# The first mixer of a two-part transformer: gelus moved into the projection, three program blocks made one, pooling sums on GpSimd

## The chip, the cores and the metric

The kernel runs on one core of one Trainium2 chip. The metric is the device time of one execution, in microseconds. The engines are TensorE (PE; its weight loads are shown as PEld), VectorE (DVE), ScalarE (ACT), GpSimd (POOL) and SyncE (SP), which here only issues DMAs.

## The reference

The program is a stack: two layers of a first model (modulated norm, a mixer, a "peer" feed-forward that picks experts), and one layer of a second model. Only the first layer's mixer is touched. Sequence length is 256 tokens, model width 1024, everything in float32. Cut to what matters here:

```python
def chunked_spatial_gating(u, v, w_s, b_s, g_v):
    vf = v.astype(jnp.float32)
    mu = jnp.mean(vf, axis=-1, keepdims=True)
    var = jnp.mean((vf - mu) ** 2, axis=-1, keepdims=True)
    vn = ((vf - mu) * lax.rsqrt(var + EPS) * g_v).astype(v.dtype)
    vn = vn.reshape(B, S // GM_CHUNK, GM_CHUNK, GM_GROUPS, GM_CH)
    w = jnp.where(causal[None], w_s, 0)
    sv = jnp.einsum('gts,bnsgc->bntgc', w, vn) + b_s.T[None, None, :, :, None]
    return u * sv.reshape(B, S, GM_WIDTH)

def multiscale_pool(p, w_pool, ls):
    ...
    for g, w in enumerate(POOL_WINDOWS):          # (2, 4, 8, 16)
        lag = cs_pad[:, POOL_MAXW - w:POOL_MAXW - w + S, sl]
        outs.append((cs[..., sl] - lag) / cnt - pf[..., sl])
    mixed = jnp.einsum('bsgc,gcd->bsgd', pooled, w_pool).reshape(B, S, POOL_WIDTH)
    return mixed * ls

# in first_block, layer 0:
mod = (c_act @ ada_w[l] + ada_b[l]).reshape(B, 6, D)[:, :, None, :]
sh1, sc1, g1, sh2, sc2, g2 = (mod[:, i] for i in range(6))
h = rmsnorm(x, norm_mix[l]) * (1 + sc1) + sh1
proj = h @ ev_w_in[e]
z = jax.nn.gelu(proj[..., :2 * GM_WIDTH], approximate=False)
ya = chunked_spatial_gating(z[..., :GM_WIDTH], z[..., GM_WIDTH:], ev_w_s[e], ev_b_s[e], ev_g_v[e])
yb = multiscale_pool(proj[..., 2 * GM_WIDTH:], ev_w_pool[e], ev_pool_scale[e])
y = jnp.concatenate([ya, yb], axis=-1) @ ev_w_out[e]
x = x + g1 * y
h = rmsnorm(x, norm_ffn[l]) * (1 + sc2) + sh2
x = x + g2 * peer(h, peer_w_q[l], peer_sub_keys[l], peer_u[l], peer_v[l])
```

The other layers compute the same as before, with the same instructions.

## The kernel before

Activations lie transposed, features on the 128 partitions and the 256 tokens along the free dimension, as 8 blocks of 128x256 (`x_T`). A big tensor `arena` holds what each stage needs. Weights are streamed in tiles of 128x1024 (512 KB) through a ring of four slots: SyncE issues the load of tile n+4 when TensorE has used tile n (`load_tile`, L249), ScalarE makes the rounded high part (`make_high`, L277), VectorE the remainder (`make_low`, L283), and TensorE multiplies with both parts. `linear` is this loop with hooks: `aside` is a generator of extra work for VectorE, one step a tile, `aside_act` the same for ScalarE, `issue` for DMAs that ScalarE issues, `behind` for loads that SyncE puts behind a given tile.

Every stage is an `nc.Block()`: one instruction stream for each engine. At its end all engines wait for each other, so a block lasts as long as its slowest engine, and nothing of the next block starts earlier. Inside a block the order on each engine is the order in which the code is written; semaphores (`wait_ge`, `then_inc`) order the engines among each other, and a `Chain` makes VectorE wait for its own instruction before.

The part of the program around the change is `even_mixer`, from 38 to 160 us:

1. `linear` over `ev_w_in`, 12 tiles. VectorE has one modulation block a tile as `aside` (a dot product of 1024 elements with the conditioning vector, L699, blocks 16 to 27). Their weights come in chunks of four blocks (2 MB each, L671): chunks 0 and 1 in the setup, chunks 2 and 3 issued behind tiles 5 and 7 of this linear.
2. A block with the gelus of u and v (L987, L988), the clearing of the gate table (8 MB of zeros written to DRAM by four DMAs, L745), the mean and variance by TensorE (L976, L981), a square root, the pooling windows (L1003 to L1014, nine instructions of adds and copies) and the mask on VectorE, a reciprocal (L1017) and the scaling of v (L1018). SyncE loads five small arrays, waits for all of them, and then issues chunks 4 and 5. Modulation blocks 28 and 29 stand first on VectorE.
3. A block (`token_major`) that turns the scaled v by eight transposes (L907), with modulation blocks 30 to 33 on VectorE.
4. A block with the spatial matmuls (L1031), the pooling matmuls (L1035), and their evictions into `cat` (L1044, L1047, L1054).
5. `linear` over `ev_w_out`, 8 tiles, with the sum of squares for the next norm and modulation blocks 34 to 39. After block 39 a bias add and a gain are computed (L684, L688).

The gate table is read and added to by the peer stage, which first needs it past 212 us. `keep_warm` issues matmuls of zeros.

## Time and profile before

| | us |
|---|---|
| runs | 2633.80, 2637.85, 2642.37 |
| median of the runs | 2637.85 |
| span of the profiled execution | 2641.4 |
| TensorE busy | 2431.8 (92%) |
| VectorE busy | 1854.0 (70%) |
| ScalarE busy | 1319.5 (50%) |
| GpSimd busy | 574.5 (22%) |

The profile gives the span, from the first to the last instruction, of one execution, and no total time of its own beside it; the slowest of the three runs is 0.97 us above that span. Times in rows are microseconds from the start of the span; the last of a row in brackets is how long the engine stood idle before it and whose event ended that. "PEq" as the releaser, with the line of a block, is the wait of all engines for each other at a block's end. A TensorE instruction in float32 on 128x256 shows as two records.

### The profile page before, as it was taken

What the parts mean: (1) busy time and instruction counts of PE and PEld (TensorE: products, weight loads), DVE (VectorE), ACT (ScalarE), POOL (GpSimd) and SP (SyncE); (2) the same over time, 40 slices, a digit from 0 to 9 for tenths busy, and PEclk for the clock granted to TensorE, in tenths of its full rate; (3) what the DMA queues carried; (4) which work ended last, traced back from release to release, by engine and by line L of the source; (5) the groups of instructions that cost most, each with busy time, mean ns of one, the idle gap of its engine ahead of it and who ended that gap; (6) DMA issues with size and microseconds to landing.
All of it is one profiled execution on the core that took longest, in us unless ns stands there. A gap on an engine that the chain in (4) does not pass through costs nothing. (4 is left out here: it accounts for less than half of the span.)

```text
span 2641.4 us, 44330 instructions
## 1 busy us (share of the span) xinstructions
PE 2431.8 (92%) x16488; PEld 2160.9 (82%) x16488; DVE 1854.0 (70%) x3808; ACT 1319.5 (50%) x2022; POOL 574.5 (22%) x392
## 2 busy tenths in 40 slices
...
GB/s 348 279 165 149 181 183 181 182 260 56 247 264 262 266 265 192 275 80 144 171 182 182 182 183 123 135 216 216 218 218 155 175 140 80 4 129 95 174 167 153
DMA packets 200513, 480.52 MB, mean 182 GB/s; under 512 B 54448, under 2 KB 87728, under 8 KB 199760
## 3 DMA queue, kind: packets, MB, share of 16 engines
...
## 5 line engine op out<-in xcount | busy, mean ns | idle before, releaser
L283 DVE TENSOR_TENSOR weight_low<-weight_raw,weight_high 128x1024 fp32r<-128x1024 f32 x732 | 893.6, 1223 | 375.2 <-ACT weight_high L277 365.1
L277 ACT ACTIVATE weight_high<-weight_raw 128x1024 fp32r<-128x1024 f32 x732 | 774.1, 1059 | 646.1 <-DMA weight_raw<-peer_v_dram 342.0
L387 PE MATMUL bank<-h_parts,weight_high 128*128 128x256 f32 x4608 | 842.7, 286 | 38.1 <-DVE h_parts L570 21.7
L387 PEld LDWEIGHTS bank<-h_parts,weight_high 128*128 128x128 f32 x4608 | 729.6, 195 | 40.3 <-issue 40.3
L387 PE MATMUL bank<-h_parts,weight_low 128*128 128x256 f32 x2304 | 657.8, 286 | 0.0
L1217 POOL DMA_INDIRECT gate_table<-pick_expo,pick_spot x256 | 475.3, 1857 | 594.4 <-DVE pick_expo L1319 379.9
L387 PEld LDWEIGHTS bank<-h_parts,weight_low 128*128 128x128 f32 x2304 | 448.6, 195 | 0.0
L394 PE MATMUL bank<-h_parts,weight_high 128*128 128x512 f32 x1120 | 400.5, 407 | 39.1 <-DVE weight_low L283 17.5
L1505 PE MATMUL bank<-weight_high,act_high 128*128 128x512 f32 x1024 | 316.0, 390 | 7.2 <-DVE act_low L1572 6.1
L1505 PE MATMUL bank<-weight_low,act_high 128*128 128x512 f32 x1024 | 315.3, 389 | 0.0
L1505 PE MATMUL bank<-weight_high,act_low 128*128 128x512 f32 x1024 | 315.2, 389 | 0.0
L396 PE MATMUL bank<-h_parts,weight_low 128*128 128x256 f32 x1120 | 297.5, 285 | 0.0
L394 PEld LDWEIGHTS bank<-h_parts,weight_high 128*128 128x128 f32 x1120 | 208.6, 193 | 91.7 <-issue 47.3
L1572 DVE TENSOR_TENSOR act_low<-arena,act_high 128x256 fp32r<-128x256 f32 x256 | 108.7, 425 | 213.1 <-ACT act_high L1539 213.0
L1505 PEld LDWEIGHTS bank<-weight_high,act_high 128*128 128x128 f32 x1024 | 191.9, 188 | 47.9 <-issue 8.4
L396 PEld LDWEIGHTS bank<-h_parts,weight_low 128*128 128x128 f32 x1120 | 217.0, 194 | 11.2
L1505 PEld LDWEIGHTS bank<-weight_low,act_high 128*128 128x128 f32 x1024 | 192.3, 188 | 40.0
L1505 PEld LDWEIGHTS bank<-weight_high,act_low 128*128 128x128 f32 x1024 | 192.3, 188 | 39.8
L1282 ACT ACTIVATE arena<-bank 128x256 f32<-128x256 f32 x256 | 97.9, 382 | 214.6 <-PE bank L387 214.1
L494 ACT ACTIVATE arena<-bank 128x256 f32<-128x256 f32 x140 | 53.2, 380 | 127.0 <-PE bank L394 126.3
L1539 ACT ACTIVATE act_high<-arena 128x256 fp32r<-128x256 f32 x256 | 102.2, 400 | 10.4 <-PEq L1368 9.6
L1661 POOL TENSOR_TENSOR arena<-arena,trig 128x512 f32<-128x512 f32 x4 | 5.4, 1380 | 467.6 <-POOLq L418 467.6
...
## 6 DMA issues: line engine op xcount, KB each, us to landing
weight_raw<-peer_u_dram SPq DMA_DIRECT2D x256, 512.0 KB
weight_raw<-peer_v_dram SPq DMA_DIRECT2D x256, 512.0 KB
...
gate_table<-kept ACTq DMA_DIRECT2D x8, 2048.0 KB, 17.4
...
kept<-gate_table SPq DMA_DIRECT2D x256, 64.0 KB, 3.4
...
```

The costliest lines, as they stand in the source:

```text
L277: self.nc.scalar.activation(self.high[:, slot, :], self.raw[:, slot, :], ACT.Identity) \
L283: eng.tensor_tensor(self.low[:, slot, :], self.raw[:, slot, :], self.high[:, slot, :].bitcast(F32), ALU.subtract) \
L387: mm = self.nc.tensor.matmul(out, w, x, start=(start and i == 0), stop=(stop and i == 2), skip_group_check=skip)
L394: wide = lambda: self.nc.tensor.matmul(bank[:], high, parts.rearrange("p s t -> p (s t)"), start=start, stop=stop, skip_group_check=True)
L396: narrow = lambda: self.nc.tensor.matmul(bank[:, 0:T], low, parts[:, 0, :], start=False, stop=False, skip_group_check=True)
L494: nc.scalar.activation(sums[:, n, :], self.bank[b][:, T:2 * T], ACT.Identity).then_inc(copied.sem, 1)
L1217: pool.indirect_dma_start(core.table[layer], bass.IndirectOffsetOnAxis(ap=b.spot[:, h, i:i + 1], axis=0), b.expo[:, 0, h, i:i + 1], None, ...
L1282: nc.scalar.activation(acts[:, n, :], core.bank[n % RING][:, 0:T], ACT.Gelu).then_inc(free.sem, 1)
L1505: mm = nc.tensor.matmul(out[2 * t + h][:], x[:, slot, of], w[:, slot, halves[h]], start=(first and n == 0), stop=(last and n == 2), skip_g ...
L1539: nc.scalar.activation(core.act_high[:, n % RING, :], acts[:, n, :], ACT.Identity).then_inc(rounded.sem, 1)
L1572: nc.vector.tensor_tensor(core.act_low[:, slot, :], acts[:, n, :], core.act_high[:, slot, :].bitcast(F32), ALU.subtract).then_inc(split.se ...
L1661: nc.gpsimd.tensor_tensor(dst[:, 2 * n:2 * n + 2, :], src[:, 2 * n:2 * n + 2, :], cosb, ALU.mult) \
```

## The change

In words:

- The first linear gets `gelus` as `aside_act`: eight gelus of 128x256, one a tile from tile 2 on, behind the copy and the high part of that tile. Each waits until VectorE has added that block. Chunk 3 is no longer loaded there.
- The three blocks behind it become one. GpSimd makes the pooling windows (two memsets, a copy and four adds). VectorE no longer copies windows, it multiplies by the counts straight from the two buffers (two instructions of 128x512). Square root and reciprocal become Ln and Exp with scale -0.5 on ScalarE. The first three weight tiles of `ev_w_out` are split into high and low parts in this block. Modulation blocks 28 and 29 stand behind the pooling work, 30 and 31 move on.
- SyncE loads the small arrays in two sets with no wait of its own, and issues chunks 3, 4 and 5 right behind.
- The second linear does not load the table for the root again (it was loaded in the block before), starts with the activations' parts at once, takes modulation blocks 30 and 31 before its tile loop (`early=2`) and one block behind each of its 8 tiles (32 to 39). ScalarE issues the clearing of the gate table there, 8 pieces of 1 MB, one a tile.
- The waits for the cleared table count the new number of DMAs. The second table is still cleared in four pieces.

The diff, cut to its core:

```diff
                     return
-                if squares is not None:
+                if squares is not None and not prepared:
                     self.prepare_root()
                 if halves is not None:
...
                 steps = iter(()) if aside is None else aside(dve)
+                for _ in range(early):
+                    next(steps, None)
                 for n in range(seg.count):
                     done = (n + 1) % groups == 0
...
+CLEARINGS = (8, 4)
+CLEARED = (16 * CLEARINGS[0], 16 * (CLEARINGS[0] + CLEARINGS[1]))
+
+
+def clearing(core, eng, layer):
+
+    parts = CLEARINGS[layer]
+    cleared, zeros = core.sig("table_cleared"), core.zeros.unsqueeze(1).to_broadcast([P, P * P // D // parts, D])
+    table = core.table[layer].rearrange("(p c n w) o -> c p n (w o)", p=P, c=parts, w=D)
     eng.wait_ge(core.sig("zeros_made").sem, layer + 1)
-    for c in range(CLEARINGS):
+    for c in range(parts):
         eng.dma_start(table[c], zeros).then_inc(cleared.sem, 16)
+        yield
 
 
...
+    def gelus(act):
+        yield
+        yield
+        for n in range(8):
+            act.wait_ge(free.sem, free.at(n + 1))
+            nc.scalar.activation(proj[:, n, :], proj[:, n, :], ACT.Gelu)
+            yield
+
     core.linear("scalar", None, sums=proj, aside=lambda dve: modulations(core, dve, range(16, 28)), norm=mixer_norm(core, 0),
-                behind={5: lambda sp: load_modulations(core, sp, 2), 7: lambda sp: load_modulations(core, sp, 3)})
+                behind={5: lambda sp: load_modulations(core, sp, 2)}, aside_act=gelus, prepare=False)
     u, v, p = proj[:, 0:4], proj[:, 4:8], proj[:, 8:12]
-    gelus = sig("gelus_ready")
...
+            for name, pairs in small_sets.items():
+                for dst, source in pairs:
+                    sp.dma_start(dst, core.dram[source]).then_inc(sig(name).sem, 16)
+            for q in range(3, 6):
                 load_modulations(core, sp, q)
 
         @block.tensor
         def _(pe):
...
                 mm = nc.tensor.matmul(var, core.c("ones"), squares[:, g, :], start=(g == 0), stop=(g == 3))
             mm.then_inc(vars_.sem, 1)
-            core.keep_warm(6)
+            core.keep_warm(3)
+            pe.wait_ge(normed.sem, normed.at(1))
+            for t in range(TT):
+                transposes(core, pe, [centred[:, g, t * P:(t + 1) * P] for g in range(4)], [core.bank[t]], turned)
+            core.keep_warm(1)
+            pe.wait_ge(masked.sem, masked.at(1))
+            for t in range(TT):
+                pe.wait_ge(kept.sem, kept.at(t + 1))
+                for g in range(4):
+                    mm = nc.tensor.matmul(core.bank[2 + t][:, g * P:(g + 1) * P], tokens[:, t, g * P:(g + 1) * P],
+                                          spatial[:, g, :], start=True, stop=True)
+                mm.then_inc(mixed.sem, 1)
+            pe.wait_ge(sig("pooling_loaded").sem, 48)
+            pe.wait_ge(pooling.sem, pooling.at(1))
+            for g in range(4):
+                mm = nc.tensor.matmul(core.bank[4 + g][:, 0:T], w_pool[:, g, :], pooled[:, g, :], start=True, stop=True)
+                mm.then_inc(pools.sem, 1)
...
-            nc.scalar.activation(v, v, ACT.Gelu).then_inc(gelus.sem, 1)
-            nc.scalar.activation(u, u, ACT.Gelu)
-            clear_table(core, act, 0)
+            core.prepare_root()
+            core.first_parts(act, "high")
...
-            nc.scalar.activation(root, var, ACT.Sqrt, bias=core.c("eps"), scale=1.0 / 512).then_inc(rooted.sem, 1)
+            nc.scalar.activation(root, var, ACT.Ln, bias=core.c("eps"), scale=1.0 / 512).then_inc(logged.sem, 1)
...
+        @block.gpsimd
+        def _(pool):
+            link = Chain(pool_step, pool)
+            nc.gpsimd.memset(ping[:, :, 0:16], 0.0)
+            nc.gpsimd.memset(pong[:, :, 0:16], 0.0)
+            link(nc.gpsimd.tensor_copy(ping[:, :, 16:], p))
+            src, dst = ping, pong
+            for g in range(4):
+                shift = 1 << g
+                i = nc.gpsimd.tensor_tensor(dst[:, g:4, 16:], src[:, g:4, 16:], src[:, g:4, 16 - shift:16 - shift + T], ALU.add)
+                if g < 3:
+                    link(i)
+                src, dst = dst, src
+            i.then_inc(windows.sem, 1)
...
+            core.first_parts(dve, "lows")
             dve.wait_ge(rooted.sem, rooted.at(1))
...
+            nc.vector.tensor_tensor(centred, centred, root.unsqueeze(1).to_broadcast(wide), ALU.mult).then_inc(normed.sem, 1)
+            dve.wait_ge(sig("spatial_loaded").sem, 32)
+            nc.vector.tensor_tensor(spatial, spatial, mask.unsqueeze(1).to_broadcast([P, 4, P]), ALU.mult).then_inc(masked.sem, 1)
+            dve.wait_ge(windows.sem, windows.at(1))
+            dve.wait_ge(sig("pooling_loaded").sem, 48)
+            counts = inv_count.rearrange("p (g t) -> p g t", g=4)
+            for first, sums in ((0, pong), (1, ping)):
+                i = nc.vector.tensor_tensor(pooled[:, first:4:2, :], sums[:, first:4:2, 16:], counts[:, first:4:2, :], ALU.mult)
+            link(i)
+            nc.vector.tensor_tensor(pooled, pooled, p, ALU.subtract).then_inc(pooling.sem, 1)
+            for _ in modulations(core, dve, range(28, 30)):
+                pass
...
-                aside=lambda dve: modulations(core, dve, range(34, 40)), squares=core.x, root=core.work[:, 0:T])
+                aside=lambda dve: modulations(core, dve, range(30, 40)), squares=core.x, root=core.work[:, 0:T], prepared=True, early=2,
+                issue=lambda act: clearing(core, act, 0))
```

What stands in the order of instructions. First VectorE between the counts of the pooling and the block that evicts the spatial products, before (L1013 and L1014 are pooling, L1015 the mask, L1017 the reciprocal, L1018 the scaling of v, L699 modulation blocks, the branches with a barrier the ends of blocks):

```order
L1013 TENSOR_TENSOR arena<-arena 128x1024 [waits small_loaded,dve_step]
L1014 TENSOR_TENSOR arena<-arena 128x1024 [waits dve_step]
L1015 TENSOR_TENSOR arena<-arena 128x512 [waits dve_step]
L1017 RECIPROCAL work<-work 128x256 [waits rooted,dve_step]
L1018 TENSOR_TENSOR arena<-arena,work 128x1024 [waits dve_step]
L964 UNCONDITIONAL_BRANCH [waits dve_step]
L937 UNCONDITIONAL_BRANCH [waits barrier_Pool_Activation_PE_DVE_SP_release]
L699 SCALAR_TENSOR_TENSOR arena,mod<-arena,kept 128x1024 [waits mod_chunk3_loaded] x2
L699 SCALAR_TENSOR_TENSOR arena,mod<-arena,kept 128x1024 [waits mod_chunk4_loaded] x2
L922 UNCONDITIONAL_BRANCH
L1038 UNCONDITIONAL_BRANCH [waits barrier_Pool_Activation_PE_DVE_SP_release]
```

and VectorE of the changed kernel from the centring of v on (L1059; L1061 squares, L283 the low parts of `ev_w_out`, L1064 the scaling of v, L1066 the mask, L1071 and L1073 pooling, L706 modulation blocks 28 and 29, L1079 the eviction of the spatial products):

```order
L1059 SCALAR_TENSOR_TENSOR arena<-bank,arena 128x1024 [waits mean_ready]
L1061 TENSOR_TENSOR arena<-arena 128x1024 [waits dve_step]
L283 TENSOR_TENSOR weight_low<-weight_raw,weight_high 128x1024 [waits high_ready] x3
L1064 TENSOR_TENSOR arena<-arena,work 128x1024 [waits rooted]
L1066 TENSOR_TENSOR arena<-arena 128x512 [waits spatial_loaded]
L1071 TENSOR_TENSOR arena<-arena 128x2x256 [waits pooling_loaded,windows_summed]
L1071 TENSOR_TENSOR arena<-arena 128x2x256
L1073 TENSOR_TENSOR arena<-arena 128x1024 [waits dve_step]
L706 SCALAR_TENSOR_TENSOR arena,mod<-arena,kept 128x1024 [waits mod_chunk3_loaded] x2
L1079 SCALAR_TENSOR_TENSOR arena<-bank,cols,arena 128x128 [waits spatial_mixed]
L1079 SCALAR_TENSOR_TENSOR arena<-bank,cols,arena 128x128 x3
L1079 SCALAR_TENSOR_TENSOR arena<-bank,cols,arena 128x128 [waits spatial_mixed]
```

The low parts have moved ahead of the scaling, pooling and two modulation blocks stand between the scaling and the eviction, and there is no barrier between them.

Next ScalarE from the last eviction of the mixer into the second linear, before:

```order
L1054 ACTIVATE arena<-bank,cols 128x256 [waits pool_mixed] x4
L1026 UNCONDITIONAL_BRANCH
L512 UNCONDITIONAL_BRANCH [waits barrier_Pool_Activation_PE_DVE_SP_release]
L348 ACT_TABLE_LOAD
L277 ACTIVATE weight_high<-weight_raw 128x1024 [waits slot0_loaded]
L525 ACTIVATE h_parts<-arena 128x2x256 x4
L277 ACTIVATE weight_high<-weight_raw 128x1024 [waits slot1_loaded]
L277 ACTIVATE weight_high<-weight_raw 128x1024 [waits slot2_loaded]
L277 ACTIVATE weight_high<-weight_raw 128x1024 [waits slot3_loaded]
L326 ACTIVATE squares<-x_T 128x256 [waits bank_free]
L277 ACTIVATE weight_high<-weight_raw 128x1024 [waits slot0_loaded]
L326 ACTIVATE squares<-x_T 128x256 [waits bank_free]
```

and in the changed kernel:

```order
L1037 ACTIVATE arena<-bank,cols 128x256 [waits pool_mixed] x4
L987 UNCONDITIONAL_BRANCH
L513 UNCONDITIONAL_BRANCH [waits barrier_Pool_Activation_PE_DVE_SP_release]
L527 ACTIVATE h_parts<-arena 128x2x256 x4
L277 ACTIVATE weight_high<-weight_raw 128x1024 [waits slot3_loaded]
L326 ACTIVATE squares<-x_T 128x256 [waits bank_free]
L754 DMA gate_table<-kept 128x2x1024 [waits zeros_made]
L277 ACTIVATE weight_high<-weight_raw 128x1024 [waits slot0_loaded]
L326 ACTIVATE squares<-x_T 128x256 [waits bank_free]
L754 DMA gate_table<-kept 128x2x1024
L277 ACTIVATE weight_high<-weight_raw 128x1024 [waits slot1_loaded]
L326 ACTIVATE squares<-x_T 128x256 [waits squares_added,bank_free]
```

The table load and the first high parts are gone from the start, and a DMA that clears a piece of the table stands behind each tile's squares.

Last VectorE at the end of the second linear, before (L335 adds squares, L635 updates x, L283 is a low part of the next linear's weights):

```order
L699 SCALAR_TENSOR_TENSOR arena,mod<-arena,kept 128x1024 [waits mod_chunk5_loaded]
L684 TENSOR_TENSOR mod<-mod,cols 128x16 [waits mod_step]
L688 SCALAR_TENSOR_TENSOR gain<-mod,cols 128x8 [waits mod_step]
L335 TENSOR_TENSOR work<-work,squares 128x256 [waits squares_added,squared,mod_step]
L635 SCALAR_TENSOR_TENSOR x_T<-bank,mod,x_T 128x256 [waits tiles_used]
L283 TENSOR_TENSOR weight_low<-weight_raw,weight_high 128x1024 [waits high_ready]
L335 TENSOR_TENSOR work<-work,squares 128x256 [waits squares_added,squared]
L635 SCALAR_TENSOR_TENSOR x_T<-bank,mod,x_T 128x256 [waits tiles_used]
L283 TENSOR_TENSOR weight_low<-weight_raw,weight_high 128x1024 [waits high_ready]
L418 UNCONDITIONAL_BRANCH
```

and in the changed kernel (the same are L335, L642 and L283):

```order
L706 SCALAR_TENSOR_TENSOR arena,mod<-arena,kept 128x1024 [waits mod_chunk5_loaded]
L335 TENSOR_TENSOR work<-work,squares 128x256 [waits squares_added,squared]
L642 SCALAR_TENSOR_TENSOR x_T<-bank,mod,x_T 128x256 [waits tiles_used]
L283 TENSOR_TENSOR weight_low<-weight_raw,weight_high 128x1024 [waits high_ready]
L706 SCALAR_TENSOR_TENSOR arena,mod<-arena,kept 128x1024 [waits mod_chunk5_loaded]
L335 TENSOR_TENSOR work<-work,squares 128x256 [waits squares_added,squared]
L642 SCALAR_TENSOR_TENSOR x_T<-bank,mod,x_T 128x256 [waits tiles_used]
L283 TENSOR_TENSOR weight_low<-weight_raw,weight_high 128x1024 [waits high_ready]
L706 SCALAR_TENSOR_TENSOR arena,mod<-arena,kept 128x1024 [waits mod_chunk5_loaded]
L691 TENSOR_TENSOR mod<-mod,cols 128x16 [waits mod_step]
L695 SCALAR_TENSOR_TENSOR gain<-mod,cols 128x8 [waits mod_step]
L419 UNCONDITIONAL_BRANCH [waits mod_step]
```

A modulation block now follows each of the last two tiles, and the bias add and the gain (L691, L695) are the last instructions of the block.

## Rows read from the trace of the kernel before

**Rows 1.** Windows view: length, busy PE, PEld, DVE, ACT, POOL; granted clock, DMA share, GB/s.

```profile
86.40:108.00 21.60, 12.77 (x32) 7.30 (x32) 16.82 (x22) 5.04 (x5) 0.00 (x0) 0.82 0.99 384
...
129.40:159.50 30.10, 28.24 (x198) 26.06 (x198) 25.80 (x41) 14.26 (x21) 0.00 (x0) 0.90 0.45 140
```

**Rows 2.** Timeline of TensorE, 86 to 129.5 us: start, length, instruction, idle before.

```profile
88.83 3.78 PE L976 MATMUL bank<-arena,const 128*128 128x256 f32 x8 [5.13 <-ACT arena L987]
...
95.18 1.99 PE L981 MATMUL bank<-arena,const 128*128 128x256 f32 x8 [0.73 <-DVE arena L1001]
...
117.75 3.75 PE L1031 MATMUL bank<-arena 128*128 128x128 f32 x16 [7.58 <-PEq L922]
...
129.38 0.55 PE L387 MATMUL bank<-h_parts,weight_high 128*128 128x256 f32 x1 [5.12 <-DVE h_parts L570]
```

**Rows 3.** Timeline of VectorE, 70 to 125 us.

```profile
70.87 1.23 DVE L283 TENSOR_TENSOR weight_low<-weight_raw,weight_high 128x1024 fp32r<-128x1024 f32 x1 [2.35 <-ACT weight_high L277]
...
92.65 1.22 DVE L999 SCALAR_TENSOR_TENSOR arena<-bank,arena 128x1024 f32<-128x1024 f32 x1 [3.81 <-PE bank L976]
...
106.46 1.22 DVE L1018 TENSOR_TENSOR arena<-arena,work 128x1024 f32<-128x1024 f32 x1
...
115.07 1.22 DVE L699 SCALAR_TENSOR_TENSOR arena<-arena,kept 128x1024 f32<-128x1024 f32 x1 [4.46 <-DMA arena<-ada_first_dram]
...
122.71 1.23 DVE L1047 TENSOR_TENSOR arena<-arena 128x1024 f32<-128x1024 f32 x1
```

**Rows 4.** Windows view in stretches of 2 us: the granted clock.

```profile
84.00:86.00 2.00, 0.00 (x0) 0.00 (x0) 2.00 (x4) 0.11 (x1) 0.00 (x0) 0.98 0.37 119
86.00:88.00 2.00, 0.00 (x0) 0.00 (x0) 1.70 (x5) 1.57 (x2) 0.00 (x0) 0.50 0.77 185
...
92.00:94.00 2.00, 2.00 (x6) 1.03 (x4) 1.32 (x2) 0.78 (x1) 0.00 (x0) 0.82 1.02 353
```

**Rows 5.** Groups of instructions on GpSimd, kept apart by shape.

```profile
L1798 POOL TENSOR_TENSOR arena<-arena,trig 128x512 f32<-128x512 f32 x8 | 12.6, 1605 | 0.0
...
L1661 POOL TENSOR_TENSOR arena<-arena,trig 128x512 f32<-128x512 f32 x4 | 5.4, 1380 | 467.6 <-POOLq L418 467.6
...
L2405 POOL COPY arena<-const 128x64 f32<-128x64 f32 x16 | 3.8, 235 | 67.2 <-ACTq L2379 67.2
...
L840 POOL MEMSET kept<- 128x1024 f32 x1 | 1.0, 951 | 0.3 <-POOLq L2906 0.3
```

**Rows 6.** Groups on VectorE, 1090 to 1110 us, beside L1798 on GpSimd.

```profile
L1825 DVE TENSOR_TENSOR arena<-arena,scratch 128x512 f32<-128x512 f32 x8 | 8.6, 1076 | 0.7 <-POOL arena L1798 0.4
L1820 DVE TENSOR_TENSOR scratch<-bank,trig 128x512 f32<-128x512 f32 x8 | 5.4, 679 | 0.0
```

**Rows 7.** One line, L1364, from 600 to 612 us: durations min/median/max, first start.

```profile
L1364 POOL TENSOR_SCALAR scratch<-const,by_pick x4: 835/855/974, 604.1 to 606.8; 128x128 f32<-128x128 f32 x4
L1364 POOLq MODIFY_POOL_CONFIG  x2: 11/12/12, 604.0 to 604.0; - x2
```

**Rows 8.** Timeline of ScalarE, 124 to 140 us.

```profile
125.02 1.28 ACT L348 ACT_TABLE_LOAD   x1 [0.26 <-PEq L1026]
...
137.97 1.06 ACT L277 ACTIVATE weight_high<-weight_raw 128x1024 fp32r<-128x1024 f32 x1 [2.61 <-DMA weight_raw<-ev_w_out_dram]
```

**Rows 9.** DMA issues, 84 to 130 us: size each, median us to landing.

```profile
gate_table<-kept ACTq DMA_DIRECT2D x4, 2048.0 KB, 19.6
arena<-ada_first_dram SPq DMA_DIRECT2D x2, 2048.0 KB, 18.3
...
arena<-ev_w_pool_dram SPq DMA_DIRECT2D x1, 256.0 KB, 11.0
```

**Rows 10.** Timeline of VectorE, 151 to 160 us.

```profile
153.71 0.17 DVE L688 SCALAR_TENSOR_TENSOR gain<-mod,cols 128x8 f32<-128x8 f32 x1
...
156.12 0.48 DVE L635 SCALAR_TENSOR_TENSOR x_T<-bank,mod,x_T 128x256 f32<-128x256 f32 x1
158.02 1.23 DVE L283 TENSOR_TENSOR weight_low<-weight_raw,weight_high 128x1024 fp32r<-128x1024 f32 x1 [1.43 <-ACT weight_high L277]
```

112 lines of the change are left out of this document (43 added, 69 removed).

## The prediction

> **What bounds the kernel now.** I read the windows view by stage first, then TensorE's, VectorE's and ScalarE's timelines of the stretch, then the DMA issues; the chain of waits of the page holds only the last instruction and is of no use. Over the whole span TensorE is the bound, but not here: from 86.4 to 108.0 us it is busy 12.77 of 21.60 us, much of it with matmuls of zeros [rows 1]. The reader is to see three waits in TensorE's timeline: 5.13 us for the gelus, 7.58 us in front of the spatial matmuls, 5.12 us before the second linear starts [rows 2]. What ends them is a serial chain through blocks that end with a wait of all engines. In the first block VectorE is the chain from 92.65 (centring) to 107.7 (end of the scaling of v), without a gap [rows 3]. In the second, TensorE's transposes are long done, but VectorE waits 4.46 us for chunk 4 of the modulation weights, until 115.07 [rows 3]: chunks 4 and 5 took 18.3 us to land, since they were issued behind small loads that SyncE waited for, and beside the 8 MB of zeros, which took 19.6 us a piece [rows 9]. The third block is evictions and one multiply that ends at 123.9 [rows 3]. The second linear then loads a table and makes high and low parts before TensorE starts at 129.38 [rows 2, 8]. So every microsecond off this chain is a microsecond off the program: nothing runs beside it that could be late, since all later stages start behind it, and the weights of the next tiles lie in their slots.
>
> **The change part by part.** All times are from the barrier B that opens the mixer's block (86.4 before).
>
> (a) The first linear. Chunk 3, 2 MB, no longer stands in SyncE's queue ahead of tile 8. VectorE waited 2.35 us for that tile's high part at 70.87 [rows 3]; from there on it has about 2.9 us of work a tile and regains the time only until TensorE's own pace binds, which it does on the last tiles. I take 0.6 us, bounds 0 and 1. The eight gelus (about 0.4 us each, the size of a 128x256 activation) and one table load of 1.28 us [rows 8] stand on ScalarE, which in this stretch waits for DMAs and for TensorE each tile; their own wait, for a block added two tiles ago, is met. Nothing queued behind them (a copy and a high part) is needed for some microseconds. Cost 0; if that cover were gone it would be the 1.28 us.
>
> (b) The mixer, B to the next barrier, 38.6 us before (86.4 to 125.0 [rows 8]). The chain now: TensorE starts 0.3 behind B instead of behind table load and gelu. Eight records of 128x256 take 1.99 us at the high clock and 3.78 at the low one [rows 2]. The granted clock was 0.98 until 86 us and 0.50 right after, with TensorE idle since before 84, and on its way back only in the stretch from 92, at 0.82 [rows 4]; the new block opens just there, so I take the low level (1.2 GHz): mean at 4.1. Centring 1.22 [rows 3], 5.4. Then five instructions with two operands in SBUF: squares 1.22, three low parts 1.2 each, scaling 1.22, mask 0.69, with gaps 6.7 us. GpSimd works beside them. Its adds of 128x512 took 1.38 to 1.61 us [rows 5]; the four adds are 4, 3, 2 and 1 times 256 columns, five such halves, 6.9 to 8.0 us. The copy of 1024 columns is not in the trace: below lies the memset of that size, 0.95 us, above 16 times the copy of 64 columns, 3.8 us [rows 5]; I take 2.0, nearer the memset, since a copy of 64 columns is mostly fixed cost. With memsets and waits the windows are ready at about 11.2, bounds 8.5 and 13.5. While GpSimd adds, VectorE's adds with two operands in SBUF took 1.08 us instead of 0.69, and those with one in PSUM stayed at 0.68 [rows 6]. I take a half more for the time of overlap, 5.4 to 11.2, which costs 1.9 us (0 to 3.5): mask ends at 14.0. The root is no part of it: variance and Ln and Exp are ready some 2 us before the low parts end. GpSimd's windows, at 11.2, are awaited at 14.0 and hidden; past that point they are late one for one. Counts twice 0.69 and subtraction 1.22: 16.7. Modulation blocks 28 and 29, 2.6 us: 19.3; before, they stood in TensorE's wait for the gelus, now on the chain. Their chunk and the small arrays ahead of it are 3.4 MB; at the 384 GB/s of that stretch [rows 1], with 2 us of latency, they are there at about 11. TensorE's transposes, ScalarE's two copies and the spatial matmuls (3.75 us at the low clock [rows 2]) are done at about 17 and fit beside it. Evictions 2.3, memset and multiply 1.35: 22.9; barrier about 0.3: 23.2. Gain 15.4 us. Bounds: high clock, no contention and a short copy 19.3, gain 19.3; windows at 17 and low clock 26, gain 12.
>
> (c) Start of the second linear, 125.02 to 129.38, 4.36 us. Table load 1.28, high part 1.06 and low part 1.22 are out of the chain; barrier, one pair of high and one of low parts of the activations stay, 1.6 us. Gain 2.8 (2.3 to 3.0).
>
> (d) End of the second linear. A modulation block (1.22 and its accumulator read, 1.3 us) now follows tile 6 too, and the bias and gain (0.17 each, 0.45 with their waits [rows 10]) leave the place before it: x of tile 7, at 156.12, comes 0.85 later. Behind the low part at 158.02 [rows 10] come one more block and the bias and gain, 1.8 us, in which only the barrier waits. Loss 2.7 (1.9 to 3.2).
>
> (e) The table's 8 MB of zeros are written beside this linear, 1 MB a tile, with 0.5 MB of weights a tile. A tile takes TensorE about 3 us (198 records in 28.24 us, 24 a tile, the first at the low clock [rows 1]); 1.5 MB in 3 us is 0.5 MB a microsecond, where queues that were never empty moved 0.38 [rows 1]. So weights land later: the high part of tile 4 waited 2.61 us for its DMA at 137.97 as it was [rows 8]. With half the bandwidth a tile lands 1 to 1.5 us later. TensorE has tiles in hand and does not stop, but VectorE's low parts shift, and with them the last update. Loss 0.8; below 0, above 5: a load of 256 KB beside the zeros took 11.0 us [rows 9], and eight weight tiles late like that would stop TensorE about twice.
>
> (f) The wait for the cleared table comes past 212 us, long after the last piece, issued before 160 and 20 us at most in landing [rows 9]: 0. The rest of the program is unchanged.
>
> Before GpSimd's first add the changed program has an instruction that configures GpSimd, as the kernel before has in front of L1364. There it took 12 ns, and the first instruction behind it started 0.1 us later [rows 7]. The Trainium skill, page "GPSIMD Engine Reference", section "Instruction dispatch", states that the first call into a freshly loaded kernel pays about 6 us with nothing in the profile. By that rule the windows would be ready at 17 instead of 11, 3 us after VectorE asks; by the row nothing is lost. The row decides, and the rule is a rival below.
>
> The sum: -0.6 - 15.4 - 2.8 + 2.7 + 0.8 = -15.3 us. Against the profiled execution: span 2641.4 becomes 2626.1. Against the median of the runs, 2637.85, which lies 4.5 below the slowest of them, the one nearest to the profile's span: 2622.5.
>
> **The rivals.**
> 1. GpSimd becomes the bound of the block: windows not at 11 but at 17, if VectorE slows the adds as they slow it: 8.0 us times 1.08 over 0.69 is 12.5, and the copy at its upper bound 3.8, with 0.5 for the rest [rows 5, 6]. For it: adds of one size took between 1.38 and 1.61 [rows 5]. Against: three microseconds of margin. Price 3 us beyond 14.0, time 2625.5; with windows at 20, 2628.5. The rule quoted above would give this case.
> 2. The zeros starve the weights. For it: 11.0 us for 256 KB [rows 9]. Against: that load stood behind 1.3 MB of others and beside pieces of 2 MB issued all at once, not one a tile. Price 5 us more than taken, and 2 more at the start of the next linear: 2629.5.
> 3. The block is better than I sum it: the high clock at its start, 1.8, and no contention, 1.9: 2618.8.
> 4. Slower than before: GpSimd's four adds, each waiting for the last, take so long that windows come later than B + 29.5. The place is VectorE's wait before the counts; it decides from 14.0 and eats the whole gain at 29.5. It would need adds at over three times the 1.61 us a half. Only a slow strided or offset operand would do that: the offset of 1 to 8 columns is in no row. Windows at 35 give 2643.5.
>
> **How the numbers follow.** Forecast 0.63, rival 1 0.12, rival 2 0.12, rival 3 0.10, rival 4 0.03. The bounds of the terms sum to -23 at best (1, 19.3, 3.0, less 1.9 and less 0, is 21.4, with a wobble of the median) and to -6 at worst (12 and 2.3, less 3.2 and 5); the runs themselves differ by 8.6 us, and a median of a few by perhaps 3. Range 2614 to 2632. What a measurement of this kernel can tell from no change is 0.3%, 7.9 us, so faster means below 2629.9: the forecast, rival 3, rival 1 but for its tail, and half of rival 2 lie there: 0.86. Same 0.11, slower 0.03.
>
> **What would show it.** In the changed profile: the mixer's block takes 23 us and has one barrier; TensorE's first mean matmul starts 0.3 us behind it at a granted clock of 0.5; the low parts in that block take 1.5 to 1.8 us each while GpSimd adds and 1.2 after; VectorE does not wait before the counts; the second linear's first matmul comes 1.6 us behind its barrier; its last instruction on VectorE is the gain. The forecast is wrong if GpSimd's last add ends over 14 us behind B, if TensorE waits for a low part in the second linear, or if the stretches behind 160 us have changed by more than 2 us in sum.

## The result and the profile after

The changed kernel took 2624.85 us (median of 7 runs, 2614.69 to 2629.70), the kernel before 2639.64 us beside it (7 runs, 2632.20 to 2645.57). The ratio is 0.9939 with a 95% interval of 0.9922 to 0.9957: 16 us or 0.6% faster (the medians differ by 14.8 us). The forecast was 2622.5 us. Timed again on another chip the ratio was 0.9942 (0.9922 to 0.9962). Ratios compare fast runs alone: one of the eight runs of e1_clear_later below took 3075.94 us at a granted clock of 0.74 and does not count in its ratio.

First the windows view of the changed kernel, for the mixer's block and for the second linear up to VectorE's first instruction of the next one; the columns are those of [rows 1].

```profile
84.60:105.30 20.70, 15.19 (x60) 10.46 (x60) 18.28 (x24) 7.98 (x13) 8.05 (x7) 0.89 0.97 366
106.80:143.70 36.90, 29.34 (x198) 26.60 (x198) 28.32 (x47) 12.71 (x20) 0.00 (x0) 0.90 0.86 338
```

The block takes 20.7 us where three blocks took 38.6. The second linear takes 37.0 us, against 30.5 from its first matmul at 129.38 [rows 2] to the next linear, and moves 338 GB/s where it moved 140 [rows 1]. The gain and the price stand in these two rows. VectorE's first instruction of the next linear, before and changed, gives the end of both:

```profile
159.88 0.88 DVE L588 SCALAR_TENSOR_TENSOR arena<-x_T,gain,work 128x256 f32<-128x256 f32 x2 [0.63 <-PEq L418]
```

```profile
143.77 0.88 DVE L593 SCALAR_TENSOR_TENSOR arena<-x_T,gain,work 128x256 f32<-128x256 f32 x2 [0.97 <-PEq L419]
```

TensorE's timeline of the changed kernel:

```profile
84.62 1.97 PE L999 MATMUL bank<-arena,const 128*128 128x256 f32 x8 [2.32 <-PEq L419]
...
90.45 3.64 PE L1004 MATMUL bank<-arena,const 128*128 128x256 f32 x8 [2.14 <-DVE arena L1061]
...
106.79 0.77 PE L387 MATMUL bank<-h_parts,weight_high 128*128 128x256 f32 x2 [4.83 <-DVE h_parts L574]
...
127.39 0.48 PE L387 MATMUL bank<-h_parts,weight_high 128*128 128x256 f32 x2 [1.20 <-DVE weight_low L283]
```

The waits of 5.13 and 7.58 us [rows 2] are gone. The mean took 1.97 us, at the high level of the clock (2.4 GHz; granted 1.00 from 84 to 90 us), the variance 3.64 at the low one (1.2 GHz; granted 0.50 from 92 to 94 us). At 127.39 TensorE stands still for a low part, which the prediction had excluded.

VectorE's timeline of the block (L1059 centres v, L1061 squares it):

```profile
86.63 1.22 DVE L1059 SCALAR_TENSOR_TENSOR arena<-bank,arena 128x1024 f32<-128x1024 f32 x1 [2.31 <-PE bank L999]
87.89 2.51 DVE L1061 TENSOR_TENSOR arena<-arena 128x1024 f32<-128x1024 f32 x1
90.32 4.86 DVE L283 TENSOR_TENSOR weight_low<-weight_raw,weight_high 128x1024 fp32r<-128x1024 f32 x3
95.10 1.21 DVE L1064 TENSOR_TENSOR arena<-arena,work 128x1024 f32<-128x1024 f32 x1
96.24 0.68 DVE L1066 TENSOR_TENSOR arena<-arena 128x512 f32<-128x512 f32 x1
96.84 1.28 DVE L1071 TENSOR_TENSOR arena<-arena 128x512 f32<-128x512 f32 x2
...
103.78 1.23 DVE L1082 TENSOR_TENSOR arena<-arena 128x1024 f32<-128x1024 f32 x1
```

It never waits after the mean. The squares take 2.51 us instead of 1.22 and the three low parts 4.86 instead of 3.5. GpSimd's part, first its timeline, then three views of the line of the adds (durations in ns: least, median, most, then the first and last start):

```profile
84.76 1.04 POOL L1044 COPY arena<-arena 128x1024 f32<-128x1024 f32 x1
85.87 7.09 POOL L1048 TENSOR_TENSOR arena<-arena 128x1024 f32<-128x1024 f32 x4
```

```profile
L1048 POOLq MODIFY_POOL_CONFIG  x2: 12/12/12, 85.7 to 85.8; - x2
L1048 POOL TENSOR_TENSOR arena<-arena x1: 1897/1897/1897, 85.9 to 85.9; 128x1024 f32<-128x1024 f32 x1
L1048 POOL TENSOR_TENSOR arena<-arena x2: 1466/1682/1897, 85.9 to 87.8; 128x1024 f32<-128x1024 f32 x1, 128x768 f32<-128x768 f32 x1
L1048 POOL TENSOR_TENSOR arena<-arena x2: 1588/1746/1905, 89.4 to 91.4; 128x512 f32<-128x512 f32 x1, 128x256 f32<-128x256 f32 x1
```

The windows are ready at 92.96, 8.4 us behind the barrier; VectorE takes them at 96.84. The adds of 1024 and 768 columns last 1.90 and 1.47 us, those of 512 and 256 last 1.91 and 1.59: the smaller ones are waiting for something. Read beside VectorE's rows it is turn-taking. The squares come at 87.89, the add of 768 columns has begun at 87.83 and ends at 89.3, and the squares end 1.1 us behind that. The add of 512 comes at 89.4, and ends 0.9 us behind the squares' end at 90.4; the first low part comes at 90.32 and ends at 92.38, 1.1 us behind the add. The pattern goes on to the last add.

The second linear on VectorE, its waits and one whole tile (132.10 to 134.77):

```profile
117.12 1.23 DVE L283 TENSOR_TENSOR weight_low<-weight_raw,weight_high 128x1024 fp32r<-128x1024 f32 x1 [1.93 <-ACT weight_high L277]
...
120.83 1.23 DVE L283 TENSOR_TENSOR weight_low<-weight_raw,weight_high 128x1024 fp32r<-128x1024 f32 x1 [0.61 <-ACT weight_high L277]
...
126.02 1.22 DVE L283 TENSOR_TENSOR weight_low<-weight_raw,weight_high 128x1024 fp32r<-128x1024 f32 x1 [2.08 <-ACT weight_high L277]
...
129.47 1.23 DVE L283 TENSOR_TENSOR weight_low<-weight_raw,weight_high 128x1024 fp32r<-128x1024 f32 x1 [0.36 <-ACT weight_high L277]
...
132.10 0.48 DVE L642 SCALAR_TENSOR_TENSOR x_T<-bank,mod,x_T 128x256 f32<-128x256 f32 x1
132.49 1.21 DVE L283 TENSOR_TENSOR weight_low<-weight_raw,weight_high 128x1024 fp32r<-128x1024 f32 x1
133.62 1.22 DVE L706 SCALAR_TENSOR_TENSOR arena<-arena,kept 128x1024 f32<-128x1024 f32 x1
134.77 0.08 DVE L706 DVE_READ_ACCUMULATOR arena<-arena,kept 128x1 f32 x1
134.77 0.42 DVE L335 TENSOR_TENSOR work<-work,squares 128x256 f32<-128x256 f32 x1
135.10 0.48 DVE L642 SCALAR_TENSOR_TENSOR x_T<-bank,mod,x_T 128x256 f32<-128x256 f32 x1
...
138.11 0.48 DVE L642 SCALAR_TENSOR_TENSOR x_T<-bank,mod,x_T 128x256 f32<-128x256 f32 x1
140.02 1.23 DVE L283 TENSOR_TENSOR weight_low<-weight_raw,weight_high 128x1024 fp32r<-128x1024 f32 x1 [1.43 <-ACT weight_high L277]
```

From 132.10 to 135.10 and on to 138.11, a tile takes VectorE 3.0 us without a gap; three matmuls of TensorE take 0.36 us here, 24 of them 2.9. VectorE has no slack left to make up a wait. The kernel before has the same 3.0 us in each tile with a modulation block, between two low parts of its second linear:

```profile
142.08 1.22 DVE L283 TENSOR_TENSOR weight_low<-weight_raw,weight_high 128x1024 fp32r<-128x1024 f32 x1
...
145.09 1.21 DVE L283 TENSOR_TENSOR weight_low<-weight_raw,weight_high 128x1024 fp32r<-128x1024 f32 x1
```

In the changed kernel the high parts wait for weights, on ScalarE, 11.5 us in four times:

```profile
ACT weight_high L277 <- DMA weight_raw<-ev_w_out_dram: 11.5, 4, 3.8
```

and the windows view shows the load on the DMA engines (share 1.02, 418 GB/s), and an idle stretch ahead of it:

```profile
106.00:108.00 2.00, 1.21 (x6) 1.24 (x7) 2.00 (x4) 2.00 (x4) 0.00 (x0) 0.50 0.17 70
108.00:110.00 2.00, 2.00 (x11) 2.00 (x11) 2.00 (x4) 0.43 (x1) 0.00 (x0) 0.50 0.00 0
...
116.00:118.00 2.00, 2.00 (x19) 2.00 (x19) 0.88 (x1) 1.37 (x2) 0.00 (x0) 1.00 1.02 418
```

The DMA view, for three single microseconds (114 to 115, 116 to 117, 118 to 119), tells the two queues apart; q1 carries the weights, q10 the zeros (packets, MB, share of the 16 DMA engines):

```profile
q1 hardware_dynamic: 75, 0.31, 90.3%
...
q10 hardware_dynamic: 101, 0.41, 100.4%
...
q1 hardware_dynamic: 102, 0.40, 97.6%
```

Here the two do not share the bandwidth evenly, they take turns: the weights of tile 5, issued at 114.70, move hardly anything before the piece of zeros issued at 112.36 is through.

### The profile page after: what moved, and what is told of

Read it like the earlier page. It is cut to its first block and busy times, and to the rows that moved or that the text cites. A ratio compares the mean times of both kernels' runs of the same rounds, so it can differ in the third digit from the quotient of the medians.

```text
span 2622.7 us, 44309 instructions
## 1 busy us (share of the span) xinstructions
PE 2425.7 (92%) x16484; PEld 2155.7 (82%) x16484; DVE 1850.0 (71%) x3797; ACT 1319.6 (50%) x2028; POOL 580.2 (22%) x399
## 5 line engine op out<-in xcount | busy, mean ns | idle before, releaser
L283 DVE TENSOR_TENSOR weight_low<-weight_raw,weight_high 128x1024 fp32r<-128x1024 f32 x732 | 894.8, 1225 | 367.8 <-ACT weight_high L277 363.4
```

Source lines behind the costliest of these rows:

```text
L283: eng.tensor_tensor(self.low[:, slot, :], self.raw[:, slot, :], self.high[:, slot, :].bitcast(F32), ALU.subtract) \
```

## The experiments

Three lengths serve below, all from the profiled executions: the block (barrier to the second linear's start), the second linear (first matmul to VectorE's first instruction of the next linear), and the next linear from there to the first scores. Behind the scores nothing differs but the run: an unchanged stretch behind the first layer's table, from GpSimd's L1364 to its memset past 1066 us (lines of the kernel before), varied between 481 and 489 us, so effects of 1 to 3 us are read from stages.

| kernel | block | second linear | next linear | all, to the scores |
|---|---|---|---|---|
| before | 40.86 | 30.50 | 52.88 | 126.34 |
| changed | 20.70 | 36.98 | 52.91 | 112.09 |
| changed, again | 20.97 | 36.55 | 53.25 | 112.27 |
| e1_clear_later | 20.97 | 33.06 | 58.18 | 113.71 |
| e2_no_adds | 19.53 | 37.02 | 53.65 | 111.70 |
| e3_early4 | 20.87 | 35.04 | 54.25 | 111.66 |
| e4_mods_first | 19.94 | 36.35 | 52.92 | 110.71 |
| e6_front_loaded | 20.97 | 36.31 | 53.63 | 112.41 |
| e7_front_early4 | 20.71 | 34.43 | 53.10 | 109.74 |
| e8_vector_windows | 23.44 | 35.42 | 53.59 | 113.95 |
| e9_zeros_323 | 20.97 | 35.19 | 54.04 | 111.70 |
| e10_zeros_early4 | 20.97 | 33.84 | 53.17 | 109.48 |
| e11_before_late | 35.41 | 33.69 | 51.92 | 123.11 |
| e12_zeros_in_block | 30.39 | 35.96 | 52.82 | 120.67 |

The last column also holds the start of the second linear (1.5 us; 2.1 where it loads a table). For before and e11 the block ends with the first high part, so that the table load of 1.28 us and 1 us of weight part are in it; counted to the barrier it was 38.6.

**The zeros one linear later (e1_clear_later).**

```
-                aside=..., prepared=True, early=2, issue=lambda act: clearing(core, act, 0))
+                aside=..., prepared=True, early=2)
...
 (peer-query linear)
-                    aside=lambda dve: angles(...), per_tile=3, norm=ffn_norm(core, layer))
+                    aside=lambda dve: angles(...), per_tile=3, norm=ffn_norm(core, layer),
+                    issue=lambda act: clearing(core, act, 0))
```

> The changed kernel, with the clearing of the first gate table moved from the second linear to the peer-query linear behind it (8 pieces of 1 MB, one behind each of its first 8 of 16 tiles). In the changed kernel the second linear takes 37.0 us from its first matmul (106.8) to the next linear's first instruction on VectorE (143.8), 30.5 before. Theory A, the zeros hold up the weights: the high parts' waits for DMA in that linear go back to about 1 to 2.6 us, TensorE does not stop in it, and it takes 33.0 to 33.5 us; the peer-query linear has more slack and loses at most 1 us; in all 3 us faster than the changed kernel. Theory B, VectorE bounds it, with a modulation block behind every tile: it stays at 36 to 37 us. Theory C, the zeros cost the same wherever weights stream: 3.7 us back there, 3 to 4 lost in the next linear, total within 1 us of the changed kernel.

Timed 2632.80 us against 2641.66 before, ratio 0.9960 (0.9946 to 0.9973). The second linear fell to 33.06 us: the zeros cost 3.9 us there (3.5 against the second profile of the changed kernel). VectorE waits for one high part behind the start, where the changed kernel has four such waits:

```profile
117.35 1.23 DVE L283 TENSOR_TENSOR weight_low<-weight_raw,weight_high 128x1024 fp32r<-128x1024 f32 x1 [1.20 <-ACT weight_high L277]
```

But the next linear rose by 4.9 to 5.3 us. The waits view of ScalarE in that linear, first of this kernel, then of the changed one (us, times, longest):

```profile
ACT weight_high L277 <- DMA weight_raw<-peer_w_q_dram: 22.3, 12, 3.4
```

```profile
ACT weight_high L277 <- DMA weight_raw<-peer_w_q_dram: 6.4, 11, 2.0
```

So the zeros are no cheaper there: theory A held for the second linear, theory C for the sum.

**Without GpSimd's adds (e2_no_adds).** The four adds are left out, and with them the pooling's window sums; a copy of one column takes their place.

```
-            for g in range(4): ... nc.gpsimd.tensor_tensor(dst..., src..., src shifted, ALU.add)
+            i = nc.gpsimd.tensor_copy(pong[:, :, 16:17], p[:, :, 0:1])
```

> The changed kernel with GpSimd's four window adds left out (a copy of one column a group stands in for them, so the pooling half of the mixer is not computed). Theory A, GpSimd and VectorE hold each other up when both read two operands from SBUF: VectorE's squares fall from 2.51 to 1.22 us, the three low parts from 4.86 to 3.5 us, and the scaling of v starts 2 to 2.6 us earlier, then bounded by the low parts or by the root. Theory B, the squares are slow for another reason (high parts on ScalarE, DMA traffic): 2.51 stays. In all, the mixer's block falls from 20.7 to about 18.3 us by A.

VectorE's timeline, and TensorE's:

```profile
90.02 1.23 DVE L1056 TENSOR_TENSOR arena<-arena 128x1024 f32<-128x1024 f32 x1
91.17 3.49 DVE L283 TENSOR_TENSOR weight_low<-weight_raw,weight_high 128x1024 fp32r<-128x1024 f32 x3
```

```profile
85.27 3.45 PE L999 MATMUL bank<-arena,const 128*128 128x256 f32 x8 [2.32 <-PEq L419]
```

Squares 1.23 and low parts 3.49: what VectorE loses in the block is GpSimd's doing, 2.65 us in the first profile. In the second profile it is 1.3 us, and e2 is to be compared with that one: in both the mean fell into the low clock. There the block shrank from 20.97 to 19.53 us, 1.4, and not to the 18.3 expected.

**Four modulation blocks ahead (e3_early4).** `early=2` becomes `early=4`.

> The changed kernel with four modulation blocks ahead of the second linear's tile loop instead of two; so none stands behind its last two tiles, as before the change. Theory A, the tail is what the last block, the bias add and the gain cost: from the last update of x to the next linear's first instruction on VectorE 5.66 us falls to 3.8, and the last update itself moves by at most 0.9 us, since late weights set its time; first matmul to next linear 37.0 to 35. Theory B, the two blocks only move: VectorE, 2.6 us later at tile 0, hands low part 3 on late and TensorE stops; 37.0 stays within 0.5.

The stage fell by 1.5 to 1.9 us, to the 35.0 expected, and the next linear gave back 1.0 to 1.3, where VectorE waited longer for high parts (7.6 us against 6.2 and 6.6). Median not timed; the profiled run was 2622.94.

**Modulation blocks 28 and 29 first (e4_mods_first).** They go back in front of the centring, their chunk back into the first linear.

```
-                behind={5: lambda sp: load_modulations(core, sp, 2)}, ...
+                behind={5: ..., 7: lambda sp: load_modulations(core, sp, 3)}, ...
 (VectorE, ahead of the wait for the mean)
+            for _ in modulations(core, dve, range(28, 30)): pass
```

> The changed kernel with chunk 3 loaded behind tile 7 of the first linear again and modulation blocks 28 and 29 first in the mixer's block, as before the change. Theory A: the two blocks, 2.6 us, fill VectorE's wait of 2.31 us for the mean and leave the chain: the mixer's block falls from 20.7 to about 18.5 us; the first linear ends 0.8 us later relative to its first tile. Theory B, with them VectorE's squares come under GpSimd's adds for longer, or the mean is late anyway, and less than 1 us is won; and the chunk costs the first linear 2 us or more.

GpSimd's and VectorE's timelines:

```profile
85.85 1.99 POOL L1044 COPY arena<-arena 128x1024 f32<-128x1024 f32 x1
87.92 8.80 POOL L1048 TENSOR_TENSOR arena<-arena 128x1024 f32<-128x1024 f32 x4
```

```profile
85.72 1.23 DVE L706 SCALAR_TENSOR_TENSOR arena<-arena,kept 128x1024 f32<-128x1024 f32 x1 [0.30 <-PEq L419]
86.87 2.05 DVE L706 SCALAR_TENSOR_TENSOR arena<-arena,kept 128x1024 f32<-128x1024 f32 x1
...
91.67 6.13 DVE L283 TENSOR_TENSOR weight_low<-weight_raw,weight_high 128x1024 fp32r<-128x1024 f32 x3
```

The block wins 0.8 to 1.0 us, not 2.2: the blocks fill the wait, but they take turns with GpSimd too. The copy comes at 85.85, behind a modulation block that runs to 86.9, and ends 1.04 us behind it at 87.84; the second modulation block ends 1.1 us behind that. Up to the block 0.9 us is lost in the first linear, where the chunk stands in the queue again, so nothing is won up to the block's end. Up to the scores the single profile is 0.5 us ahead with that loss counted in, too little to tell.

**Zeros into the idle stretch (e6_front_loaded), and with four blocks ahead (e7_front_early4).** Both timed with the changed kernel (e5_after_again) on one chip.

```
+            for _ in range(4): next(pieces)       # ScalarE, behind the copies of the tokens
...
-                issue=lambda act: clearing(core, act, 0))
+                issue=spread)                     # one piece at tiles 1, 3, 5, 7
```

> The changed kernel itself once more, timed on the same chip as the three kernels beside it. Expected: 2625 us, 14 to 18 us below the kernel before; the second linear 37 us from its first matmul to VectorE's first instruction of the next linear, that linear 53 us to the scores. It is the yardstick for what is won or lost below, and it shows by how much an unchanged stage differs from run to run.

> All 8 MB of zeros stay between the mixer's block and the end of the second linear, but four of the eight pieces are issued by ScalarE inside the mixer's block, behind its two copies of the tokens, so that they fall into the stretch of 106 to 114 us in which the DMA engines stood idle; the other four follow at every second tile. Theory A (the loss of the second linear is a queue of 1 MB of zeros a tile beside 0.5 MB of weights, and not the zeros as such): with half as many a tile the bandwidth suffices, ScalarE's waits for weights shrink from 13.2 us to under 5, and the second linear falls from 37.0 to 33.5 to 34.5 us, the next linear stays at 53: 2.5 to 3.5 us below the changed kernel timed beside it. Theory B (the rival: any zeros in front of the weights delay them, here those of the first tiles, which VectorE needs for its low parts at once): the waits only move to the first tiles, the stage stays at 36.5 to 37.5 and the time within 1 us. Theory C: the four early pieces delay chunks 4 and 5 of the modulation weights, and the block becomes longer than 21.5 us.

> The zeros as in the run before this one, and four modulation blocks instead of two ahead of the second linear's tile loop. With only the latter, the stage lost 1.9 us and the next linear gave 1.3 back, since the DMA queues bounded both. Theory A (the low parts of the next linear were late only since the zeros had pushed the weights back): with the queue relieved both add up: second linear 32 to 33 us, next one 53, 4 to 5 us below the changed kernel. Theory B (the next linear is bound by its own weights whatever is in front): again 1 to 1.5 us given back there, and a total within 1 us of the run before.

The changed kernel again 2625.92 us (8 runs), e6 2628.16 (9 runs, ratio to before 0.9952, 0.9936 to 0.9968), e7 2623.15 (6 runs, 0.9942, 0.9919 to 0.9965): these medians don't tell the three apart. In the stages e6 won nothing. ScalarE's and VectorE's timelines of e6:

```profile
119.85 1.06 ACT L277 ACTIVATE weight_high<-weight_raw 128x1024 fp32r<-128x1024 f32 x1 [5.65 <-DMA weight_raw<-ev_w_out_dram]
```

```profile
120.94 1.23 DVE L283 TENSOR_TENSOR weight_low<-weight_raw,weight_high 128x1024 fp32r<-128x1024 f32 x1 [4.32 <-ACT weight_high L277]
```

The other tiles waited for nothing (but for the last low part, 1.43 us in every kernel). One wait of 4.3 us in place of four with 5.0 in sum, and the stage was as long: rival theory B holds. The wait is for the weights of tile 4, issued at 113.25; from 113 to 117 us the queue of the zeros took 97% of the DMA engines and that of the weights 5%. With two more modulation blocks ahead of the tile loop (e7) the stage fell to 34.4 and the next linear gave nothing back: x of the last tile came only 0.4 us earlier, since the wait was still 3.84 us, and the tail behind it was 1.4 shorter. That is 2.4 to 2.5 us below the changed kernel, half of the 4 to 5 expected.

**Windows on VectorE (e8_vector_windows).** The copy and the four adds, with the same operands, stand on VectorE behind the mask.

> The one block stays, but the copy and the four adds of the pooling windows stand on VectorE again, behind the mask; GpSimd does its two memsets alone. It prices GpSimd's part. Theory A (GpSimd saves VectorE 4.1 us of windows and costs it 2.6 in slower squares and low parts, of which the wait for the root would keep 1.2): squares at 1.2 us, three low parts at 3.5, the block 23.4 us if the mean is taken at the high clock and 24 at the low one, against 20.7. Theory B (the slowing costs as much as the windows save): 20.7 or less. Stages behind it unchanged, 37.0 and 53.

The block took 23.44 us, near theory A, which had 24 for the mean at the low clock, as it was here. The second linear took 35.4, 1.1 to 1.6 less, so that GpSimd's part is worth 2.5 to 2.7 us in the block and 1.7 to 1.9 up to the scores.

**Zeros placed by what waits (e9_zeros_323), and with four blocks ahead (e10_zeros_early4).** As e6 and e7, with three pieces early, one at each of the tiles 1, 3, 5 and two behind the last.

> The eight pieces of zeros are placed by what VectorE waits for: three in the mixer's block, behind the two copies of the tokens (3 MB for the idle stretch of the DMA engines before the weights of tile 3 are issued), one behind each of the tiles 1, 3 and 5, two behind the last tile, where the next linear's weights are in their slots. Theory A (VectorE has 3.0 us of work a tile here, as TensorE has, so that each of its waits adds to the stage one for one, and the run with four early pieces only gathered the waits of four tiles into one of 4.3 us at tile 3, since 2 MB of zeros were still ahead of its weights at 113): now tile 3 waits 1.2 to 2 us and the others not at all, the second linear takes 33.2 to 34 us instead of 36.5 to 37, the next one 53: 2.5 to 3.3 us below the changed kernel (2625.9 on the last chip). Theory B (total bytes decide, wherever the pieces stand): the stage stays at 36 to 37. Theory C: the two last pieces delay the peer keys and the next linear's weights, and it gives back 1 us or more there.

> The same placing of the zeros, and four modulation blocks ahead of the tile loop, two of them in the time in which VectorE waits for tile 3. Theory A: both add, the second linear 31.5 to 32.5 us, the next one 53 to 53.5, 4.5 to 5 us below the changed kernel: about 2621. Theory B (the next linear's low parts, bound by their weights, take the gain back): as the run beside it, within 1 us.

e9 took 2627.59 us (5 runs, ratio 0.9961, 0.9947 to 0.9975), e10 2624.50 (6 runs, 0.9938, 0.9922 to 0.9954). The low part of tile 4 (the expectations count it as tile 3) still waited 2.74 us in e9 and that of tile 6 0.40; the stage fell by 1.4 to 1.8, half of what was expected, and the next linear gave back 0.8 to 1.1. In e10 the sum to the scores is 109.48, 2.6 to 2.8 us below the changed kernel where 4.5 to 5 were expected, the best of the stages measured; the medians can't show so little.

**The kernel before with only the zeros moved (e11_before_late).**

```
 (mixer's first block)
-            clear_table(core, act, 0)
 (second linear)
+                issue=lambda act: clearing(core, act, 0))
```

> The kernel before, with one thing alone of the change: the first table's clearing stands no longer in the mixer's first block, but in the second linear, eight pieces of 1 MB, one a tile. It tells what the zeros' place is worth by itself. Theory A: VectorE's wait of 4.46 us for chunk 4 of the modulation weights goes and the stretch from the mixer's block to the second linear's start falls from 38.6 to 34.2 us; in the second linear the zeros make VectorE wait for high parts 3.8 us in sum, of which one idle tile of VectorE (it has 6 modulation blocks for 8 tiles) takes up 1.2 to 2.5: the stage rises from 30.5 to 32 or 33; net 2 to 3 us won. Theory B (VectorE's slack takes up all): 30.5, net 4.4 won. Theory C (the zeros cost as much there as in the block): net 0.

The wait of 4.46 us for chunk 4 went; the block fell by 5.45 us, the second linear rose by 3.19, with VectorE waits for high parts of 1.74, 0.62 and 2.06. Net 3.2 up to the scores, a little more than theory A's 2 to 3. Its single run lasted 2648.70 us, longer than before's median of 2639.18; at the scores it was 3.0 us ahead of the profile of before, at the end 5.5 behind, and the stages between have the same instructions.

**The changed kernel with the zeros in the block (e12_zeros_in_block).**

```
 (mixer's block, ScalarE)
             core.first_parts(act, "high")
+            for _ in clearing(core, act, 0): pass
```

> The changed kernel with its eight pieces of zeros issued all at once near the start of the mixer's block, where the kernel before had them. It tells what the later place is worth inside the change. Until the block's end at B + 21 the DMA engines then have 16 MB in their queues, 38 us at 420 GB/s, beside 3.4 MB of small arrays and chunk 3. Theory A (the two queues share evenly, as in the kernel before): the small arrays and chunk 3 land at 16 to 19 us behind the barrier instead of 8 to 11, VectorE waits 1 to 4 us in the block for the counts or chunk 3, and chunks 4 and 5 and the weights of tile 3 come late in the second linear: block 22 to 25 us against 20.7 to 21.0, second linear 36 to 39 against 36.6 to 37.0, from block to scores 1 to 6 us longer than the changed kernel's 112.1 to 112.3. Theory B (what the zeros cost later they cost no more here, since the linear is relieved of them): block to scores within 1 us of 112.2. Theory C (as C, with the block covered by its own chain): shorter than the changed kernel by 1 to 3 us.

All three theories set it too low: 8.4 to 8.6 us more up to the scores, and the block is 9.4 to 9.7 us longer. ScalarE's and VectorE's timelines:

```profile
90.18 8.24 ACTq L754 DMA_DIRECT2D gate_table<-kept  x4
98.46 0.47 ACT L1031 ACTIVATE work<-bank,const 128x256 f32<-128x256 f32 x1 [8.00 <-issue]
```

```profile
99.42 1.23 DVE L1066 TENSOR_TENSOR arena<-arena,work 128x1024 f32<-128x1024 f32 x1 [2.61 <-ACT work L1033]
...
110.62 1.22 DVE L706 SCALAR_TENSOR_TENSOR arena<-arena,kept 128x1024 f32<-128x1024 f32 x1 [6.91 <-DMA arena<-ada_first_dram]
```

VectorE waits 6.91 us for chunk 3, and 2.61 for a root that ScalarE could have begun at 94.1: it was still issuing zeros, four pieces in 8.24 us. The second linear, free of new zeros, is hardly shorter (35.96): VectorE waits 4.86 us in it for the high part of tile 4.

## Why the prediction was right, step by step

The direction, the size and the place were right: 15.3 us forecast, 16.1 gone at the start of the next linear (159.88 to 143.77), of which 1.0 was there ahead of all edits. But that the size fits so well is luck: the block won 2.5 us more than forecast, the zeros cost 3.1 more, and the two cancelled. Two of the three signs that the prediction named for being wrong came: TensorE waited for low parts in the second linear (1.20 and 0.35 us), and the stretches behind 160 us changed by 2.6 us. The first belongs to (e), the second to (f). The third did not: the last add ends 8.4 us behind B, the barrier that opens the mixer's block.

(a) First linear: 0.6 forecast. The 2.35 us wait is gone and VectorE ends 1.84 us earlier, of which 1.0 is there already at ScalarE's first copy (49.56 against 48.54), ahead of all edits: 0.8. VectorE's work in a tile there is 2.6 us (its low parts in a row start 2.61 apart), not the 2.9 that the prediction took; TensorE's pace of 2.8 is what binds.

(b) The mixer's block: 15.4 forecast, 17.9 measured (17.6 in the second profile). Mean and clock: the forecast had the mean ready at B + 4.1 at the low clock; the first profile had it at 2.0. That was luck of the run: in ten other runs the mean took 3.16 to 3.65 us, and then the variance 1.99. TensorE pays for the low clock once, at one place or the other. The block hardly feels it (20.70 against 20.97): what the earlier mean won in the first profile, 1.6 us, VectorE lost again for the most part to GpSimd's adds, of which more were then still to come. Contention: 1.9 forecast, 2.65 measured in the first profile, 1.3 in the second (squares 2.00, low parts 4.01). Windows: ready at B + 8.4 against 11.2, since the copy took 1.04 us against 2.0, nearer still to the memset [rows 5], and the add of 128x512 took 1.04 in the second profile, where it began 0.1 us ahead of the squares and they waited for it, against 1.38 to 1.61 [rows 5]. Being hidden, this brought nothing. The mask ended at B + 12.3 (12.6 in the second profile) against 14.0. The rest of the difference is that I added durations: 1.22 us instructions of VectorE that do not depend on each other start 1.14 apart, as the three low parts in 3.49 us show, and I put gaps of 0.04 beside them. Of the 2.5 us by which the block beat the forecast (23.2 less 20.7) the mean is 2.1, contention takes back 0.8, and this leaves about 1.2 us for the overlap of some twenty instructions.

(c) Start of the second linear: 2.8 forecast, 2.86 measured (4.36 to 1.50).

(d) End of the second linear: loss 2.7 forecast. The zeros out of the way (e1), x of tile 7 comes 27.39 us behind the first matmul against 26.74, 0.65 (0.85 forecast), and the tail from there on 5.67 against 3.76, 1.9 (1.8 forecast).

(e) The zeros: loss 0.8 forecast, 3.9 measured by e1 (3.5 by the second profile). This is the mis-sized term, and it was wrong twice. First the weights: "with half the bandwidth a tile lands 1 to 1.5 us later". From SyncE's issue to the high part the tiles 4 to 7 took 3.5 us each before and in e1; in the changed kernel they took 4.2, 5.0, 7.3 and 7.9. They stand behind whole pieces of zeros, and the lateness grows from tile to tile. Then the price: the step saw that the low parts shift, but counted this once. VectorE's waits for high parts add up to 5.0 us, 3.8 more than the 1.20 of e1, and each stays, because with a modulation block behind every tile VectorE works 3.0 us a tile against TensorE's 2.9. The slack could have been worked out: low part, modulation block, update of x and sum of squares take 3.0 us in the tiles of before. e6 is the test: a single wait of 4.32 us, 3.1 more than e1's, and a stage 3.25 us longer. In all nine profiles with two blocks ahead of the tile loop x of the last tile comes 25.0 to 25.2 us behind the first matmul, plus VectorE's waits for high parts and for TensorE. In the kernel before, with two tiles free of a modulation block, the zeros still cost 3.2 (e11), so even that slack is small.

(f) The wait for the cleared table and the rest: 0 forecast; the next linear took 52.91 against 52.88. The span ends 18.7 us earlier, 2.6 more than at that point, which lies within what unchanged stages vary (the stretch of 481 to 489 us took 487.1 in the profile of before and 481.4 in that of the changed kernel).

The rivals. GpSimd never bounded the block; VectorE's request came 3.9 us behind it. The 6 us for the first call that the Trainium skill, page "GPSIMD Engine Reference", section "Instruction dispatch", states did not show: the first add starts 0.1 us behind the instruction that configures GpSimd. The zeros' rival was half true: TensorE stopped for 1.20 and 0.35 us and the stage lost 3 us more than taken, where the rival had 5, but nothing was lost at the start of the next linear. The better block came about: in the first profile mostly by the earlier mean, as the rival had it; in the second, with the mean at the low clock, by 0.45 us of the mean, 0.6 of contention and 1.2 of overlap.

What the change's parts are worth is not a sum. Moving the zeros is worth 3.2 us in the kernel before (e11) and 8.4 to 8.6 in the changed one (e12): the shorter block asks for chunk 3 earlier than it can come beside 8 MB of zeros. GpSimd's windows are worth 1.7 to 1.9. Each of these three figures rests on one profile. The other 4 of the 14.1 us up to the scores are the merged block, its prepared parts and all the rest together; they were not taken apart, so what the removed barriers are worth by themselves is not shown.
